# A two-layer backbone block: one modulation chunk gathered behind the attention instead of ahead of it

## The reference, cut to what matters

```python
s_c = jax.nn.silu(c)
for i in range(DEPTH):                      # DEPTH = 2
    mod_l = jnp.split((s_c @ ada_w[i] + ada_b[i])[:, None, :], 6, axis=-1)
    h_l = modulate(rmsnorm(x_l, norm_mix_g[i]), mod_l[0], mod_l[1])
    ...                                     # i = 0: attention and mLSTM; i = 1: 2-D DFT
    x_l = x_l + mod_l[2] * o_l
    f_l = modulate(rmsnorm(x_l, norm_ffn_g[i]), mod_l[3], mod_l[4])
    y_l = grouped_moe(f_l, router_w, router_b, exp_w_gate[i], exp_w_up[i], exp_w_down[i])
    x_l = x_l + mod_l[5] * y_l
return rmsnorm(x_l, final_g)
```

## Time and profile before

| | us |
|---|---|
| median of 3 runs | 877.04 |
| lowest, highest | 876.54, 883.07 |
| the profiled execution | 878.16 |
| its span, first to last instruction | 876.3 |
| PE busy | 750.4 (86%) |
| DVE busy | 399.3 (46%) |
| ACT busy | 154.6 (18%) |
| POOL busy | 32.7 (4%) |
| mean DMA rate | 346 GB/s |

### The profile page before, as it was taken

One profiled execution on the slowest core, in us unless ns is written; L12 is line 12 of the kernel. 1 busy time (PEld: TensorE's weight loads), 2 busy tenths in 40 slices (PEclk: granted clock), 3 DMA queues, 4 the chain that ended last, 5 costly groups with the idle time before them and its releaser, 6 DMA issues.

```text
span 876.3 us, 19160 instructions
## 1 busy us (share of the span) xinstructions
PE 750.4 (86%) x7522; PEld 436.1 (50%) x7523; DVE 399.3 (46%) x1058; ACT 154.6 (18%) x337; POOL 32.7 (4%) x58
## 2 busy tenths in 40 slices
PE   8999999998888999966758985799899679597774
PEld 4544647454554455543336752474565445374342
DVE  3368888899767752311112241533723213032335
ACT  4121012315762211000000000330300100000001
POOL 0200000111000000000000001000000000000010
PEclk9999999999998999998779997899999879799987
DMA  9998997999505689799999899996899999999961
GB/s 333 357 387 302 378 350 261 374 338 373 214 1 190 251 342 421 296 399 419 421 420 422 336 421 418 394 413 281 307 344 422 418 418 421 423 420 423 418 279 50
DMA packets 81779, 303.57 MB, mean 346 GB/s; under 512 B 9072, under 2 KB 16288, under 8 KB 57072
## 3 DMA queue, kind: packets, MB, share of 16 engines
q1 hardware_dynamic: 67456, 282.29, 81.4%
q0 software_dynamic: 3552, 12.59, 3.8%
q10 hardware_dynamic: 10704, 7.75, 2.8%
HBM read 291.19 MB, written 14.68 MB: 349 GB/s over the span
## 4 chain that ended last, share of the span: by engine, by line
PE 57%; DMA 21%; DVE 10%; issue 4%; SPq 3%; ACT 3%; ACTq 0%; DVEq 0%
DMA raw<-in_w_up 18%; PE bank L1974 17%; PE bank L1988 8%; PE bank L1955 5%; DVE bias L971 4%; PE bank L1896 3%; PE bank L1770 3%; PE bank L1784 3%; PE bank L1780 3%; PE bank L2182 3%; DMA ring<-in_w_in 3%; PE bank L1775 2%; PE bank L1789 2%; SPq L507 2%; PE bank L1673 1%
## 5 line engine op out<-in xcount | busy, mean ns | idle before, releaser
L1974 PE MATMUL bank<-raw,arena 128*32 128x256 f32 x3392 | 224.0, 417 | 73.4 <-DMA raw<-in_w_up 42.8
L1974 PEld LDWEIGHTS bank<-raw,arena 128*32 128x32 f32 x3392 | 129.3, 119 | 160.0 <-issue 113.4
L1488 DVE TENSOR_TENSOR arena<-arena,bank 128x128 f32<-128x128 f32 x53 | 15.3, 288 | 277.3 <-ACT arena L869 277.3
L1988 PE MATMUL bank<-raw,arena 128*32 128x256 f32 x1696 | 112.8, 403 | 12.4 <-issue 12.4
L1988 PEld LDWEIGHTS bank<-raw,arena 128*32 128x32 f32 x1696 | 65.9, 117 | 50.6 <-issue 25.4
L869 ACT ACTIVATE arena<-bank 128x128 f32<-128x128 f32 x53 | 14.7, 277 | 353.7 <-PE bank L1974 353.6
L1780 PE MATMUL bank<-ring,arena 128*128 128x512 f32 x160 | 69.7, 594 | 0.9 <-DMA ring<-in_w_in 0.9
L1955 PE MATMUL bank<-arena 128*32 128x256 f32 x912 | 60.9, 380 | 7.3 <-DVE arena L1455 7.3
L971 DVE SCALAR_TENSOR_TENSOR bias<-ring,small,bias 128x512 f32<-128x512 f32 x77 | 57.9, 752 | 2.7
L1780 PEld LDWEIGHTS bank<-ring,arena 128*128 128x128 f32 x160 | 30.1, 190 | 38.2 <-issue 38.1
L971 DVE SCALAR_TENSOR_TENSOR arena<-ring,small,arena 128x512 f32<-128x512 f32 x63 | 47.4, 752 | 2.2
(11 more groups left out here) (270 smaller groups left out, 787.4 us busy)
## 6 DMA issues: line engine op xcount, KB each, us to landing
raw<-in_w_gate SPq DMA_DIRECT2D x64, 1024.0 KB, 20.6
raw<-in_w_up SPq DMA_DIRECT2D x64, 1024.0 KB, 22.2
raw<-in_w_down SPq DMA_DIRECT2D x64, 1024.0 KB, 22.7
ring<-in_ada_w SPq DMA_DIRECT2D x24, 2048.0 KB, 14.5
ring<-in_w_in SPq DMA_DIRECT2D x7, 2048.0 KB, 14.2
unit_results<-arena ACTq DMA_DIRECT2D x220, 32.0 KB, 5.8
ring<-in_w_out SPq DMA_DIRECT2D x2, 2048.0 KB, 25.5
ring<-in_w_fnet SPq DMA_DIRECT2D x2, 2048.0 KB, 18.3
```

Source lines behind the costliest of these rows:

```text
L1974: ins = mm(ps[4][j * S:(j + 1) * S, 0:2 * FW].rearrange("p (m n) -> p m n", m=2), xT[:, k, :], w[:, k % 4, :, j * FW:(j + 1) * FW], start= ...
L1988: ins = mm(ps[5][j * S:(j + 1) * S, 0:XW], hT_e[:, k, :], w[:, k % 2, j * XW:(j + 1) * XW], start=(k == 0), stop=(k == KF - 1))
```

## The change

```diff
-ADA_AFTER = {n: 4 + i for i, n in enumerate((0, 2, 4, 5, 6, 7, 8, 9, 11, 12, 14, 16, 17, 18, 19, 20, 21))}
+ADA_AFTER = {n: 4 + i for i, n in enumerate((0, 2, 4, 5, 6, 7, 8, 9, 11, 12, 14, 16, 17, 18, 19, 20))}
 FILL_AFTER = 4 + len(ADA_AFTER) - 2
 ADA_LATE = range(4 + len(ADA_AFTER), 2 * N_ADA)
```

## The result

The changed kernel takes 879.13 us (median of 20 runs, 875.39 to 885.54) against 875.87 us (median of 20 runs, 868.95 to 883.15) for the kernel before, measured beside it: the ratio is 1.0051, 95% interval [1.0028, 1.0075], which is +4.5 us with +2.5 to +6.6. The medians alone are 3.3 us apart. The forecast of +2.7 us and its median of 879.7 lie inside the interval; the sign was right, the size somewhat low. The profiled span grew from 876.3 to 882.3 us.

What follows compares the result with a forecast made beforehand. VectorE ends last at the attention's start, 1.2 us behind TensorE; TensorE at the output projection's end. -1.2 + 6.17 - 1.88 - 0.99 = +2.1, plus 0.6 for the clock: +2.7 us, median 879.7; range 875.8 to 882.5.

Steps and rivals of the forecast that it cites:

- (a): Attention's start: removing eight VectorE instructions (6.17 us) gains only 1.2 us, since TensorE's first scores bound it.
- (b): Behind the attention: the same eight instructions add 6.17 us; the wait for chunk 21's save stays 2.5 us.
- (c): Gathers behind the attention: chunk 22's bias row, loaded after chunk 20, costs nothing, 2.5 us as upper end.
- (d): DMA queues: first expert's load waits for chunk 20 until about 272, fills delay a bias row and save; cost nothing.
- (e): Output projection's end: VectorE's idles of 1.88 and 0.99 us absorb part of the longer gathers; sum +2.1 us.
- (f): Routing: TensorE's 3.3 us idle brings a half-clock stretch beginning between 303 and 308; +0.6 us, between -0.8 and +2.5.
- the late save: Rival, gathers behind the attention: chunk 21's save or chunk 22's bias row lands late; +2.5 us, 882.2 us, chance 0.12.
- the long stretch at half clock that reaches into the first expert: Rival, routing into first expert: the clock costs +2.5 us in place of +0.6; 881.6 us, chance 0.15.
- the hiding by the weight stream: Rival, experts: the DMA weight stream sets their pace and absorbs the 2 us of lateness; 877.0 us, chance 0.10.
- The early save: Rival, ahead of chunk 23: chunk 21's save lands within one chunk, saving 2.5 us; 876.6 us, chance 0.08.
- the last sign of being wrong: First expert to end: the forecast is wrong if lateness at the first expert isn't that at the end.

Runs made afterwards that it cites:

- e1: Changed kernel with chunk 20 behind the attention cut to one of its eight instructions; ratio 0.9992, -0.7 us against the kernel before.
- e5: Changed kernel with GpSimd's four fills back behind chunk 19 (`FILL_AFTER` 19); one execution, 876.04 us.
- e6: Changed kernel with a place of its own for chunk 23, so it doesn't wait for chunk 21's save; ratio 1.0027, +2.4 us against the kernel before.
- e7: Changed kernel with six unread matmuls in TensorE's idle time ahead of the routing; ratio 1.0052 against the kernel before.
- e9: Changed kernel with chunk 23's own place and three unread matmuls ahead of the routing; ratio 0.9996, -0.4 us against the kernel before.
- e3: Kernel before with chunk 21 gathered three times over behind the attention (16 more instructions); ratio 1.0140, +12.3 us.
- e10: Kernel before with two unread matmuls ahead of the transposes of `mg`; ratio 0.9977, -2.0 us.
- e12: Kernel before, unchanged, profiled a second time; sum of stages 128.67 us, no timed comparison.
- e2: Kernel before with chunk 21 gathered twice over behind the attention (eight more instructions); ratio 1.0102, +8.9 us.
- e4: Kernel before with chunk 20 gathered twice over ahead of the attention (eight more instructions); ratio 1.0086, +7.5 us.
- e14: Kernel before with two of chunk 20's eight instructions moved into the attention, plus two unread matmuls ahead of `mg`'s transposes; ratio 0.9963, -3.2 us.

## Why the prediction was right, point by point

(a) The gain ahead of the attention: predicted 1.2 us with the bound at TensorE's scores, measured 17.57 - 16.57 = 1.0 by the stages; the maxima wait for TensorE in all six traces without the chunk there (changed, e1, e5, e6, e7, e9). The bound is the same in all six to 0.01 us, and lies 1.18 us behind the start of the scores, not 1.06 as predicted. With the whole chunk in its old place the stage itself varies, from 17.17 (e3) to 18.32 (e10), so the gain is anything from 0.6 to 1.8. Right.

(b) The gather behind it: predicted +6.17 with the same wait of 2.5 us; the stage grew by 27.14 - 21.15 = 5.99. Right. e6 adds that this wait is on the path, as e12 shows for the kernel before: there too the fourth residual follows the gathers without waiting for the projection.

(c) The bias row of chunk 22: predicted free. In the changed kernel chunk 22 starts without a wait; its row was issued at 274.0 and landed in 5.2 to 5.4 us, against 5.8 us from issue to use. In e1, where only 0.8 us stand in the place of a chunk, the same kind of row cost 0.94 us. Right, with little to spare.

(d) Queues: SP's first expert load was issued at 273.73 and followed chunk 20 as foreseen, and no wait comes from the fills (e5). One sign didn't come: the DMA rate in the attention was to be near nothing, and it was 114 GB/s from 205 to 266, against 148 before. What moved out is the 2 MB of the first expert; the other loads of the ring run on there. It changed nothing in the sum.

(e) The cover: this is the term that was mis-sized. The forecast subtracted 1.88 + 0.99 = 2.87 us of idle time. They were real in that trace but came from a stretch at half clock in TensorE's transposes and projection, and the argument took them for a property of the order. In the repeated profile the cover is 0.05 us. The rows that would have told were in the profile before: the two halves of the projection, 32 matmuls each by the rows' count, took 16.44 and 14.00 us. With them the sum would have had two ends, +2.1 and +4.9 before the clock, and not one. The changed kernel's own signs say the same: the projection ended at 298.6 and not 300.1, and TensorE idled for 5.92 us and not 3.3.

(f) The clock: predicted +0.6 with the half-clock stretch moved ahead into the routing; 18.80 - 18.15 = +0.65 and the stretch from 302 to 308. Right in size as a difference; the stretch began a little earlier than foreseen (303 to 308), while TensorE still stood idle. The "six matmuls" of 4.36 and 2.82 us in this step are three, counted twice each by the row, which leaves the comparison as it is. What it costs in itself is more, 1.7 us (e7), since the kernel before pays 1.1 there too.

So the mechanism was right but for one term, and the closeness of the numbers is partly luck. With a cover of 0.05 us the same working gives +5.5 us, and the stages then differ by 5.0. The forecast median of 879.7 met 879.13 also because it was added to 877.04, the median of three runs; that of twenty was 875.87.

The rivals: the late save did not come about (2.32 us of waiting), nor the long stretch at half clock that reaches into the first expert; the hiding by the weight stream is excluded by e2 and e3. The early save would have been worth what e6 shows, 2.4 us, and would not have been bounded by the projection at 1.2 us, since VectorE was last by far.

What stays open: what decides whether the output projection has its stretch at half clock. It stood in the profile before and in e4, and in none of the others, though all but e10 and e14, where matmuls fill it, have the same idle of some 1.86 us ahead of the transposes. And the time from the first expert to the end, 551.4 to 559.1 us over all these traces, varies more than the whole effect, with no relation to the order (551.4 and 556.9 for the same kernel). So the last sign of being wrong, a lateness at the end unlike that at the first expert (4.9 us against 2.7 in this pair of traces), can't be read from one pair. The spread goes with the clock: of the 75 executions of the kernel before that were timed beside the experiments, the 24 with a mean granted clock of 0.933 or less took 877.6 us on average, and the 21 with 0.939 or more 871.6. Which of the two is the cause of the other, no run shows.

## What to carry to other kernels

Where two engines finish 1 us apart, taking 6 us from the later one gains 1 us, and putting 6 us onto it costs 6: find the second runner before moving work, and move only as much as reaches it. Before an idle time is counted as cover, look whether the work that it waits for ran at full clock and has the same length twice. A chunk in a chain needs a hole of its own size only if it can't be split; two of eight instructions in an idle stretch within the attention brought the first maxima to TensorE's bound. And before a variant is called as good as the kernel before, give the kernel before the same improvements.

## What the runs showed of the hardware that was not expected

One kernel, profiled twice, had its output projection at 16.44 + 14.00 us and at 14.00 + 14.00 us, with the idle time of 1.86 us ahead of the transposes the same in both. At the attention's start an idle of 1.23 us was followed by a granted clock of 1.00 in e1 and e5, and by matmuls of 2.08 us where those have 1.13 in e7 and e9. An idle of 5.92 us (3.50 in e6) was followed by 1.94 us for eight transposes that took 1.09 us where matmuls filled the gap. Where a whole chunk stands between, the wait for the save of 256 KB varied from 1.74 to 2.67 us. An added chain of eight instructions ahead of the attention (e4) left TensorE idle for 8.38 us; the granted clock fell within that idle and stood at 0.50 for some 10 us, and the attention took 62.3 us in place of 61.3.
